# A seven-product down projection: who moves the rows of the weight sums, and in what order the products run

## The reference, cut to what matters

```python
hmix = rmsnorm(x); proj = hmix @ w_in                  # ssm input, q, k, v, gate a, gate b
y_a = (gelu(s5_scan(u)) @ glu_w_val) * sigmoid(gelu(s5_scan(u)) @ glu_w_gate)
y_b = attention(q, k, v) @ w_attn_up                   # three dilated patterns, merged
x = x + (sigmoid(gate_a) * y_a + sigmoid(gate_b) * y_b) @ w_out
hf = rmsnorm(x)
ff = (gelu(causal_dwconv(hf @ ffn_w_gate)) * (hf @ ffn_w_up)) @ ffn_w_down    # 2816 inner channels
return x + ff
```

## Time and profile before

| what | value |
|---|---|
| median of 3 runs | 1829.37 us (1826.04 to 1829.44) |
| the profiled execution | 1828.78 us, span 1827.0 us |
| mean granted TensorE clock | 0.979 |
| PE busy | 1739.7 us, 95% |
| POOL busy | 921.9 us, 50% |
| DVE busy | 1041.0 us, 57% |
| ACT busy | 663.6 us, 36% |
| chain that ended last | PE 73%, DMA 8%, DVE 7%, POOL 7% |

### The profile page before, as it was taken

One profiled execution on the slowest core, in us unless ns is written; L12 is line 12 of the kernel. 1 busy time (PEld: TensorE's weight loads), 2 busy tenths in 40 slices (PEclk: granted clock), 3 DMA queues, 4 the chain that ended last, 5 costly groups with the idle time before them and its releaser, 6 DMA issues.

```text
span 1827.0 us, 23362 instructions
## 1 busy us (share of the span) xinstructions
PE 1739.7 (95%) x8316; PEld 1389.4 (76%) x8316; DVE 1041.0 (57%) x1525; ACT 663.6 (36%) x1263; POOL 921.9 (50%) x688
## 2 busy tenths in 40 slices
PE   8999999999999978999787899999999999997998
PEld 6777777777777767888566788788888888886887
DVE  6444553555564474543212332588788787735898
ACT  6653454465355321112200122353333333342443
POOL 7544464453543375651457854345545555443553
PEclk9999999999999989999898999999999999998999
DMA  4112311321321244545345534523223223364344
GB/s 173 36 42 48 102 63 30 106 76 42 87 65 48 61 115 105 129 115 175 138 184 194 186 116 140 182 93 97 76 69 103 69 71 124 127 230 138 127 136 136
DMA packets 89689, 198.83 MB, mean 109 GB/s; under 512 B 16560, under 2 KB 34096, under 8 KB 89600
## 3 DMA queue, kind: packets, MB, share of 16 engines
q1 hardware_dynamic: 72160, 167.12, 28.8%
q10 hardware_dynamic: 16976, 28.92, 4.9%
q0 software_dynamic: 464, 1.62, 0.2%
HBM read 152.31 MB, written 44.12 MB: 108 GB/s over the span
## 4 chain that ended last, share of the span: by engine, by line
PE 73%; DMA 8%; DVE 7%; POOL 7%; issue 3%; ACT 2%; ACTq 1%; SPq 0%; DVEq 0%; POOLq 0%
PE bank L1046 11%; PE bank L1048 11%; PE bank L1047 10%; PE bank L1399 7%; PE bank L1401 7%; PE bank L1400 7%; DMA ws<-in_wblocks 4%; PE bank L1463 3%; PE bank L1464 3%; PE bank L1465 3%; PE bank L1181 2%; DMA ab<-wgt_scr 2%; PE bank L1192 2%; PE bank L1165 1%; DMA raw<-in_wblocks 1%
## 5 line engine op out<-in xcount | busy, mean ns | idle before, releaser
L1046 PE MATMUL bank<-hhi,whi 128*128 128x512 f32 x1024 | 422.0, 412 | 31.8 <-POOL wlo L759 23.5
L1047 PE MATMUL bank<-hlo,whi 128*128 128x512 f32 x1024 | 408.0, 398 | 0.0
L1048 PE MATMUL bank<-hhi,wlo 128*128 128x512 f32 x1024 | 407.6, 398 | 0.0
L759 POOL TENSOR_TENSOR wlo<-raw,whi 128x1024 fp32r<-128x1024 f32 (+1 forms) x84 | 195.4, 2326 | 355.9 <-DVE whi L1859 354.3
L1046 PEld LDWEIGHTS bank<-hhi,whi 128*128 128x128 f32 x1024 | 195.4, 191 | 82.0 <-POOL wlo L759 26.5
L1048 PEld LDWEIGHTS bank<-hhi,wlo 128*128 128x128 f32 x1024 | 195.3, 191 | 46.4
L1047 PEld LDWEIGHTS bank<-hlo,whi 128*128 128x128 f32 x1024 | 195.9, 191 | 39.9 <-issue 0.2
L1035 POOL TENSOR_TENSOR dwlo<-dw_raw,dwhi 128x512 fp32r<-128x512 f32 x77 | 106.9, 1390 | 125.9 <-ACT dwhi L1751 125.9
L1463 PE MATMUL bank<-dahi,dwhi 128*128 128x512 f32 x308 | 122.0, 396 | 11.7 <-DVE dalo L2310 11.7
L1591 ACT ACTIVATE sp<-sp,sd 128x128 f32<-128x128 f32 (+1 forms) x192 | 84.3, 440 | 116.3 <-DVE sd L2039 116.1
L1464 PE MATMUL bank<-dalo,dwhi 128*128 128x512 f32 x308 | 121.5, 394 | 0.0
(11 more groups left out here) (309 smaller groups left out, 3759.4 us busy)
## 6 DMA issues: line engine op xcount, KB each, us to landing
raw<-in_wblocks SPq DMA_DIRECT2D x76, 512.0 KB, 4.4
pair<-in_wblocks SPq DMA_DIRECT2D x40, 512.0 KB, 4.9
ws<-in_wblocks ACTq DMA_DIRECT2D x22, 512.0 KB, 5.8
wsum_scr<-ws ACTq DMA_DIRECT2D x22, 512.0 KB, 3.1
ff_scr<-ffo SPq DMA_DIRECT2D x22, 512.0 KB, 5.8
dw_raw<-wsum_scr SPq DMA_DIRECT2D x44, 256.0 KB, 2.7
ff<-ff_scr SPq DMA_DIRECT2D x36, 256.0 KB, 3.7
dw_raw<-in_wblocks SPq DMA_DIRECT2D x33, 256.0 KB, 2.9
```

Of the source, the lines that this page charges most:

```text
L759: pool.tensor_tensor(wlo[par][:, 0:cols], raw[par][:, 0:cols], whi[par][:, 0:cols].bitcast(F32), ALU.subtract).then_inc(lo_done, 1)
L1046: nc.tensor.matmul(ps, a, x, start=start and k == k_list[0], stop=False)
L1047: nc.tensor.matmul(ps, a, y, start=False, stop=False)
L1048: last = nc.tensor.matmul(ps, b, x, start=False, stop=stop and k == k_list[-1])
```

## The change

1. `load_rows` and `store_sums` go from the ACT queue to the SP queue. In gate A's round m SP issues the raw load of block m + 2, then `load_rows(m - 1)`, then (m > 1) `store_sums(m - 2)`, which waits for POOL's sum; in value/gate's round m: `zb2`, the raw load, `load_rows(7 + m)`, `store_sums(6 + m)`. POOL's sums start a round later: six in gate A (m = 2 to 7), five in value/gate (m = 0 to 4).
2. The order of the products is now 1, 2, 3, 6, 7, 5, 4: three products of plain activation quarters first.
3. DVE's activation sums are no longer three steps ahead in step order but have steps of their own: the two for products 6 and 3 in steps 16 to 36, the one for product 4 in steps 37 to 47, the one for product 5 in steps 48 to 58. The `ff` rows arrive in four groups of loads (steps 12 to 21 of SP, two a step) instead of one of 4 and one of 14 rows.
4. Two of the four output quarters (12 and 22) are finished from one bank: `tiles_22_12` scales product 5's bank once and adds it to two bases, `a12` and `s17`, which were scaled and given their residual before (`scaled`). Residual halves are loaded in four consecutive steps each.
5. Stores of those eight tiles are issued after SP's loop.

```diff
-D_AHEAD = 3
-M_1, M_2, M_6, M_7, M_5, M_4, M_3 = range(7)
+M_1, M_2, M_3, M_6, M_7, M_5, M_4 = range(7)
...
-            for n in range(2, KC + 2):
-                load(B_E2 + n, wblocks[48 + n], n % 2)
+            def load_rows(c):
+                if c >= 2:
+                    sp_.wait_ge(ws_out[c % 2], 32 * (c // 2))
+                for k in range(2):
+                    sp_.dma_start(ws[c % 2][:, k, :], wblocks[116 + NK * k + c]).then_inc(ws_in[c % 2], 16)
+            def store_sums(c):
+                sp_.wait_ge(ws_done, c + 1)
+                for k in range(2):
+                    sp_.dma_start(wsum_scr[k, c], ws[c % 2][:, k, :]).then_inc(ws_out[c % 2], 16)
+            sp_.wait_ge(state_done, HP)
+            sp_.wait_ge(osplit, HP)
+            for m in range(KC):
+                load(B_E2 + m + 2, wblocks[50 + m], m % 2)
+                if m:
+                    load_rows(m - 1)
+                if m > 1:
+                    store_sums(m - 2)
...
                 sp_.dma_start(zb2[:], zb_scr[m]).then_inc(zb_in, 16)
                 load(B_VG + m + 2, wblocks[58 + m], m % 2)
+                if KC - 1 + m < NK:
+                    load_rows(KC - 1 + m)
+                if KC - 2 + m < NK:
+                    store_sums(KC - 2 + m)
...
-            for g, h, rows, t0 in ((4, 0, range(15, 22), 8), (5, 1, range(11, 15), 12),
-                                   (6, 1, (4, 15, 5, 16, 6, 17, 7, 18, 8, 19, 9, 20, 10, 21), 16)):
+            for g, h, rows, t0, per in ((4, 0, range(15, 22), 8, 2), (5, 1, range(11, 15), 12, 2), (6, 1, (4, 15, 5, 16), 15, 2),
+                                        (7, 1, (6, 17, 7, 18), 17, 2), (8, 1, (8, 19, 9, 20, 10, 21), 19, 2)):
...
-            for g, t0, step in ((0, 23, 3), (1, 46, 2), (2, 65, 2), (3, 60, 1)):
+            for d, h, t0 in ((0, 0, 23), (0, 1, 44), (1, 1, 54), (1, 0, 58)):
...
             for m in range(KC):
                 lo(B_E2 + m + 1, (m + 1) % 2)
-                if m:
-                    weight_sums(m - 1)
+                if m > 1:
+                    weight_sums(m - 2)
             for m in range(KC):
                 lo(B_VG + m + 1, (m + 1) % 2)
-                if KC - 1 + m < NK:
-                    weight_sums(KC - 1 + m)
+                if KC - 2 + m < NK:
+                    weight_sums(KC - 2 + m)
...
-                elif q == M_6:
+                elif q == M_3:
                     pe.wait_ge(down_snap, m + 1)
-                elif q > M_6:
-                    pe.wait_ge(down_read, 4 * (q - M_7) + m + 1)
+                elif q > M_3:
+                    pe.wait_ge(down_read, 4 * (q - M_6) + m + 1)
...
+            def tiles_22_12(m):
+                product_in(M_5, m)
+                if m == 0:
+                    dve.wait_ge(out_done, 16 * 4)
+                link(TT(osb[:, m, :], dbank(M_5, m), half(rs1[:], 1), ALU.mult))
+                TT(s17[:, m, :], s17[:, m, :], osb[:, m, :], ALU.add).then_inc(out_ready, 1)
+                TT(a12[:, m, :], a12[:, m, :], osb[:, m, :], ALU.add).then_inc(out_ready, 1)
...
+            for c in range(NK):
+                at.setdefault(16 + 2 * c, []).append((sums_3_2, c))
+                at.setdefault(37 + c, []).append((sum_4, c))
+                at.setdefault(48 + c, []).append((sum_1, c))
             for m in range(4):
-                at[26 + 3 * m] = finish_tile, m
-                at[37 + m] = partial, M_6, m
-                at[48 + m] = partial, M_7, m
-                at[58 + 2 * m] = finish_tile, 4 + m
-                at[65 + m] = last_base, m
-                at[70 + 2 * m] = finish_tile, 8 + m
+                at.setdefault((25, 29, 33, 35)[m], []).append((tile_11, m))
+                at.setdefault(37 + m, []).append((partial_3, m))
+                at.setdefault(47 + m, []).append((partial_6, m))
+                at.setdefault(51 + 2 * m, []).append((scaled, a12, a12, 0, 1, m))
+                at.setdefault(59 + m, []).append((partial_7, m))
+                at.setdefault(63 + m, []).append((scaled, s17, s_2, 1, 1, m))
+                at.setdefault(67 + 2 * m, []).append((scaled, s_2, s_2, 1, 0, m))
+                at.setdefault(70 + 2 * m, []).append((tiles_22_12, m))
```

More of the change, by code:

```diff
@@ L141, in bass_hybrid_block @@
             seed = sb("seed", [P, NGROUP // 2, 2])
+        with ExitStack() as s:
+            sb = tensors(s)
+            a12 = sb("a12", [P, 4, HT])
         sb = tensors(ctx)
@@ L399, in down_act, with x1_part @@
             return b_part(c, *{M_1: (0, 0), M_2: (1, 0), M_6: (0, 0), M_7: (0, 1), M_5: (0, 1), M_4: (1, 0), M_3: (1, 1)}[q])
[L401 to L405, removed]
+        def x1_part(d, m, h):
+            return half((x1a, x1b)[d][:, m, :], h)
         def half(ap, h):
@@ L699, in load_dw, with load_x1r, store_out @@
                 sp_.dma_start(dw_raw[:, t % RING, :], down_weight(t)).then_inc(dw_in[t % RING], 16)
[L701 to L708, removed]
+            def load_x1r(d, h, m):
+                sp_.dma_start(x1_part(d, m, h), half(x1_scr[4 * d + m], h)).then_inc(x1r_in[2 * d + h], 16)
+            def store_out(n, d, h, tile):
+                m = (n - 4) // 2 if 4 <= n < 12 else n % 4
                 sp_.wait_ge(out_ready, n + 1)
-                sp_.dma_start(half(out[m + (4 if 4 <= n < 12 else 0)], h), tile).then_inc(out_done, 16)
+                sp_.dma_start(half(out[4 * d + m], h), tile).then_inc(out_done, 16)
             last_unit = SLOTS * (NU - 1)
@@ L748, in _ @@
                     f(*args)
-            for n in range(8, 16):
-                store_out(n)
+            for m in range(4):
+                store_out(4 + 2 * m, 1, 1, s17[:, m, :])
+                store_out(5 + 2 * m, 0, 1, a12[:, m, :])
+            for m in range(4):
+                store_out(12 + m, 1, 0, osb[:, 4 + m, :])
             sp_.wait_ge(out_done, 16 * 16)
@@ L1667, in _ @@
                 act.activation(yhi[:, q, :], gt[:, q % 2, :], ACT.Copy).then_inc(ysplit_hi, 1)
[L1669 to L1680, removed]
             def z_hi(k):
@@ L1702, in _ @@
                     act.activation(sg2[:, h, :], bank[4 + h][:], ACT.Sigmoid).then_inc(sgt_done, 1)
[L1703 to L1706, removed]
             z_hi(KC - 1)
@@ L1759, in down_act_hi @@
                 if q in (M_6, M_5, M_4):
-                    act.wait_ge(da_sum, {M_6: 0, M_5: NK, M_4: 2 * NK}[q] + c + 1)
+                    act.wait_ge({M_6: da_sum, M_5: da_sum5, M_4: da_sum4}[q], c + 1)
                 if t >= RING:
@@ L2310, in down_act_lo, with quarters @@
                 TT(dalo[:, t % RING, :], down_act(t), dahi[:, t % RING, :].bitcast(F32), ALU.subtract).then_inc(da_lo, 1)
[L2312 to L2324, removed]
+            def quarters(c):
+                return [b_part(c, k, h) for k in range(2) for h in range(2)]
@@ new lines, in sums_3_2, with sum_4 @@
+            def sums_3_2(c):
+                if c in (0, 4, 6, 8):
+                    g = {0: 5, 4: 6, 6: 7, 8: 8}[c]
+                    dve.wait_ge(ff_in[g], ff_in0[g] + 16 * (6 if c == 8 else 4))
+                b11, b12, b21, b22 = quarters(c)
+                link(TT(b12, b22, b12, ALU.subtract))
+                TT(b11, b11, b12, ALU.add).then_inc(da_sum, 1)
+            def sum_4(c):
+                b11, b12, b21, b22 = quarters(c)
+                dve.wait_ge(da_sum, c + 1)
+                TT(b21, b21, b11, ALU.subtract).then_inc(da_sum4, 1)
@@ L2326, in product_in, with sum_1 @@
+            def sum_1(c):
+                b11, b12, b21, b22 = quarters(c)
+                dve.wait_ge(da_lo, NK * M_7 + c + 1)
+                TT(b12, b22, b11, ALU.subtract).then_inc(da_sum5, 1)
             def product_in(q, m):
                 dve.wait_ge(*((down_tile, 3 * q + m + 1) if m < 3 else (down_used, NK * (q + 1))))
[L2329 to L2337, removed]
-                    dve.wait_ge(down_snap, 4)
[L2339 to L2362, removed]
+            def tile_11(m):
+                product_in(M_2, m)
+                if m == 0:
+                    dve.wait_ge(x1r_in[0], 16 + 64)
+                    dve.wait_ge(down_snap, 4)
+                TT(osb[:, m, :], dbank(M_2, m), s17[:, m, :], ALU.add).then_inc(down_read, 1)
+                dve.wait_ge(down_read, m + 1)
+                link(TT(osb[:, m, :], osb[:, m, :], half(rs1[:], 0), ALU.mult))
+                TT(osb[:, m, :], osb[:, m, :], x1_part(0, m, 0), ALU.add).then_inc(out_ready, 1)
@@ new lines, in partial_3, with partial_6, partial_7 @@
+            def partial_3(m):
+                product_in(M_3, m)
+                TT(a12[:, m, :], s17[:, m, :], dbank(M_3, m), ALU.add).then_inc(down_read, 1)
+            def partial_6(m):
+                product_in(M_6, m)
+                dve.wait_ge(down_read, 4 + m + 1)
+                link(TT(a12[:, m, :], a12[:, m, :], dbank(M_6, m), ALU.add))
+                TT(s_2[:, m, :], s17[:, m, :], dbank(M_6, m), ALU.add).then_inc(down_read, 1)
+            def partial_7(m):
```

(20 more changed lines are left out.)

28 lines of the change are left out of this document (9 added, 19 removed).

## The result

The changed kernel takes **1776.16 us** (median of 4 runs, 1775.30 to 1777.13) against 1828.79 (4 runs): ratio 0.9715, 95% interval 0.9698 to 0.9732. The profiled execution took 1776.18 us, its span is 1774.4 us. The forecast of 1776 was met. It was met partly by luck: two of its terms are off by some 5 us each, with opposite signs.

What follows compares the result with a forecast made beforehand. PE, busy 95% of the span, was taken as the bound, so gains come from its gaps: 43.6 + 11.2 = 54.8, less 1 unplaced, 53.8 off 1829.4 gives 1776 us; forecast range 1768 to 1784, 8-in-10 range 1765 to 1792.

Steps and rivals of the forecast that it cites:

- The 50.0 us of the front and the 16.3 of the down projection: Time PE was said to lose to gaps and slow matmuls in gate A plus value/gate, and in the down projection.
- part one: Gate A and value/gate: SyncE moves rows, sums one round later; claimed gain 43.6 us, bounds 50.0 and 30.
- Gate A without a gap: Gate A: wlo ahead of the sum ends 5 us before PE needs it, so the 10.54 us gap goes.
- The loop through SP's wait for the sum: Gate A: sum, store, raw landing, cast, wlo, sum take 9.4 us + landing, in 22.2; binds from a 12.8 us landing.
- The value/gate residue: Value/gate: waits for wlo of 0.8, 2.8 and about 1.3 us, plus 1.5 of slow clock; 6.4 us left.
- The two DVE waits of the down projection: Down projection: waits for ff rows and x1a halves go with earlier loads, worth 15.4 us.
- The new waits for DVE: Down projection: DVE lateness replaces the old waits: 2.0 us, 1.6 of slow clock, 1.5 in steps 63 to 76; residue 5.1.
- part two: Down projection: plain products first, earlier loads; 16.3 less residue 5.1 gives 11.2 us, bounds 16.3 and 3.
- The bank: Down projection, product 6: PE's fourth bank needs tile 3 read in DVE's step 35, when PE is at step 33.
- Rival 2: Gate A and value/gate: the move does nothing, POOL waits as long for ws; 1818 us, chance 0.05.
- Rivals 1, 3 and 4: SP's order binds, 1788 us, 0.11; down projection edits give nothing, 1787, 0.10; DVE/POOL lock makes it slower, 1840, 0.02.
- Rival 5's floor: Whole kernel: nothing is left of the gaps, 1829.4 - 66.3 = 1763 us; chance 0.06.

Runs made afterwards that it cites:

- e1: Kernel before with only the gate A and value/gate edits (SyncE moves rows, sums one POOL round later), down projection unchanged; 1792.3 us.
- e2: Kernel before with only the down projection edits, rows of the weight sums still moved by ScalarE; 1814.7 us.
- e3: Changed kernel, but ScalarE issues the rows of the weight sums again; POOL's sums stay one round later; 1775.7 us.
- e4: Changed kernel, but SyncE loads rows one round earlier and POOL sums as before the change: seven in gate A, four in value/gate; 1772.8 us.
- e5: Changed kernel, but seven sums in gate A and value/gate's four in rounds 0, 2, 4 and 6; 1766.6 us.
- e8: Changed kernel, but in value/gate the sigmoids and t2 of a block come before the hi copy and lo part of the previous z; 1771.8 us.
- e6: Kernel before with only earlier loads of ff rows and tile 0's residual halves in the down projection; 1814.8 us.
- e7: Changed kernel with two more useless DVE operations, in steps 32 and 34 of the down projection; 1778.1 us.

## Why the prediction was right, point by point

**Where the loss lay: right.** The 50.0 us of the front and the 16.3 of the down projection were the pool from which everything came, and their causes were those named: POOL waiting for ws in front of wlo, and DVE waiting for ff rows and x1a halves. e1 and e2 show that they are separate. The remedy of the front was more than enough: part one changes the queue and POOL's round, and e3 and e4 show that one of the two will do.

**Gate A without a gap: right.** 292 matmuls in 67.5 us. The loop through SP's wait for the sum did not bind. One ws landing took 10.2 us (the longest that the forecast had seen was 8.1), still under the 12.8 from which it would bind.

**The value/gate residue: mechanism half right, size wrong.** The forecast said 6.4 us lost, with wlo as PE's release in blocks 4 to 6; it was 11.9. The step that failed is "PE wants blocks 4, 5 and 6 ... and gets them" when wlo is done. POOL's rounds of 14.3 us do set the pace (e4, e5), but PE is released by t2, which the program puts behind the hi copy and the lo part of the z before. The earlier trace rows show PE waiting for wlo; the same view of before also has this row, and the forecast did not use it:

```profile
PE bank L1046 <- DVE t L2171: 11.8, 5, 4.0
```

e8 takes the chain away and gives what the forecast described, waits for wlo, two of them, with 97.6 us for value/gate, 3.4 less. So the chain explains 3.4 of the 5.5 us that are missing. The rest was mis-sized: POOL's rounds with a sum take 14.2 to 14.4 us in the changed kernel, not the 13.9 "because its rows now come early", and behind e8's wait of 2.79 us fourteen matmuls run at the slow pace, 2.9 us where the forecast had 1.5. It is chance that three of the changed kernel's four waits (0.78, 2.80, 1.26 and 2.88 us) look like the forecast's 0.8, 2.8 and 1.3: they are waits for t2, and each stands a block earlier. So part one gave 38.1 instead of 43.6.

**The two DVE waits of the down projection: right.** They are gone, and e6 shows that loading earlier does it: 13.6 us.

**The new waits for DVE: the mechanism exists, the size was wrong.** The term "I take 2.0 and 1.6 of slow clock ... 1.5 for this part" should have been 0, so part two gave 16.5 instead of 11.2. The bank was the right one. Between tile 1's read-out and tile 3's, DVE in the changed kernel does 16 operations with SBUF inputs and 2 with PSUM in 18.05 us: (18.05 - 2 x 0.69)/16 = 1.04 us each, inside the 0.9 to 1.09 that I weighed. Tile 3 is read here:

```profile
1649.57 1.79 DVE L2312 TENSOR_TENSOR dalo<-ff,dahi 128x512 fp32r<-128x512 f32 x1
1651.29 0.68 DVE L2347 TENSOR_TENSOR osb<-bank,s 128x512 f32<-128x512 f32 x1
```

PE wants the bank at 1560.71 + 33 x 2.72 + 9 x 0.227 = 1652.5. DVE is done at 1651.97, 0.5 us early. The forecast put this read-out 2.0 us late, 2.5 from where it came, and had to have it to half a us; e7 shows that two operations more would have made it true: they move the read-out by 2.9 us against the start of the stage. The other part of the term, 1.5 us for steps 63 to 76, was 0 as well: PE has no break there either (busy for 30.49 of the last 30.50 us). The Trainium skill (SBUF — State Buffer, Who interferes with whom) says that a DVE operation with two SBUF inputs and a GpSimd (POOL) operation that reads SBUF exclude each other, the loser waiting for the whole of the other. The trace agrees: 1.79 us for the dalo above, which starts inside this POOL operation and outlasts it by 0.5 us, beside 0.68 for the operation with a PSUM input.

```profile
1649.25 1.57 POOL L1060 TENSOR_TENSOR dwlo<-dw_raw,dwhi 128x512 fp32r<-128x512 f32 x1 [0.87 <-ACT dwhi L1753]
```

**The other rivals.** Rival 2 (the move does nothing) did not happen, but e3 shows that with the sums a round later the change of queue adds nothing, and e4 that with the change of queue the later round adds nothing to gate A. The Trainium skill (DMA: Bandwidth & Descriptors, Issuing engines are not separate DMA queues) says that transfers of all issuing engines interleave on the same DMA engines, and the trace agrees: e3's ws landings have a median of 3.8 us, the changed kernel's 4.0. Rivals 1, 3 and 4 did not happen. Rival 5's floor, 1763, is nearly reached by e5 (1766.6).

## What to carry to other kernels

When a helper engine does both urgent work (the lo part that the matmul waits for) and early work for a later stage, see to it that the early work finds its loads landed: issue them ahead of the wait for the piece of work before, or do the work a round later. Once that held, it did not matter here which queue issued them. An extra piece of work that makes a round longer than the matmul's block should stand in every second round, so that the next one catches up. When forecasting what is left, list every release of the waiting engine, not only the one with the most waiting time, and follow each to its end: the second one may be later.

## What the runs showed of the hardware

How much does a PE gap cost beyond its own length? Take every gap of more than 0.25 us in front (860 to 1080) and in the down projection, in all eleven traces, and the distances between the starts of the matmuls behind it: 0.23 us at full pace, 0.42 to 0.43 in a slow stretch.

| gap, us | gaps | with a slow stretch behind | matmuls in it | extra time, us |
|---|---|---|---|---|
| 0.33 to 1.98 | 32 | 0 | | |
| 2.21 to 10.54 | 35 | 34 | 6 to 14 | 1.3 to 2.9 |

The extra time doesn't grow with the gap: it is 1.7 us behind one of 2.21 us (e7), 2.9 behind one of 2.79 (e8), and 1.6, 1.7 and 2.7 behind the three of 10.54 (e2, before, e6). The slow stretch starts with the gap's first matmul or up to six matmuls later. The one exception is a gap of 2.65 us in e6. So a gap of a little over 2 us costs nearly twice its length here (e7: a wait of 2.2 us, the eight matmuls behind it start 0.38 to 0.59 us apart, and the stage takes 4.1 us more), one of 1.98 us (e8) only itself. These are counts of what happened; no run varied the length of a gap alone. The chip's two clock levels are 1.2 and 2.4 GHz. By stretch, e7 has a granted clock of 0.74 in the 6.6 us behind its wait and 1.00 after:

```profile
1653.40:1660.00 6.60, 6.38 (x21) 5.15 (x22) 6.50 (x10) 2.12 (x4) 1.52 (x1) 0.74 0.35 117
1660.00:1700.00 40.00, 40.00 (x178) 33.13 (x177) 38.59 (x41) 16.56 (x30) 20.33 (x15) 1.00 0.40 139
```
